# Expert tiles of 64 rows, with two 64-column matmuls side by side, and Pool copies that signal semaphores, in a two-layer MoE trunk

## The reference

```python
def grouped_moe(x, w_router, b_router, w_e_in, w_e_out):
    ...
    expert = g_sel[:, None] * EXPERTS_PER_GROUP + top_i     # two of 16 experts for each token
    weight = top_p / jnp.sum(top_p, axis=-1, keepdims=True)
    flat_e = expert.reshape(-1)
    order = jnp.argsort(flat_e)
    tok = order // TOP_K
    xs = xt[tok]
    group_sizes = jnp.bincount(flat_e, length=N_EXPERTS).astype(jnp.int32)
    h = lax.ragged_dot(xs, w_e_in, group_sizes)             # 1024 -> 2 x 512
    h_gate, h_up = jnp.split(h, 2, axis=-1)
    y = lax.ragged_dot(jax.nn.silu(h_gate) * h_up, w_e_out, group_sizes)   # 512 -> 1024
    y = y * weight.reshape(-1)[order][:, None].astype(y.dtype)
    out = jnp.zeros_like(xt).at[tok].add(y.astype(xt.dtype))
    return out.reshape(B, S, D)
```

## Time and profile before

| | |
|---|---|
| median of 3 runs | 3080.5 us (3073.62 to 3087.33) |
| the profiled execution | 3085.13 us, span 3083.4 us |
| busy share: PE, DVE, ACT, POOL | 91%, 51%, 38%, 9% |
| matmuls | 15876 |
| mean granted TensorE clock | 0.952 |
| data moved | 398.58 MB, 129 GB/s on the mean |

### The profile page before, as it was taken

One profiled execution on the slowest core, in us unless ns is written; L12 is line 12 of the kernel. 1 busy time (PEld: TensorE's weight loads), 2 busy tenths in 40 slices (PEclk: granted clock), 3 DMA queues, 4 the chain that ended last, 5 costly groups with the idle time before them and its releaser, 6 DMA issues.

```text
span 3083.4 us, 47529 instructions
## 1 busy us (share of the span) xinstructions
PE 2802.9 (91%) x15876; PEld 1464.4 (47%) x15877; DVE 1561.9 (51%) x2494; ACT 1162.9 (38%) x1846; POOL 267.5 (9%) x240
## 2 busy tenths in 40 slices
PE   5999999999999599999579999999999995999994
PEld 3555554554444344454345555555544442544452
DVE  3243463344346666656533345633433466577665
ACT  3234413222232166546432444232222321566563
POOL 0000000000000022222310000000000000222223
PEclk8999999999999699999788999999999996999996
DMA  6200001111115488877622000111111254699874
GB/s 254 69 1 28 28 19 51 35 46 41 52 62 198 147 310 306 307 246 258 222 77 69 28 1 28 35 35 35 52 52 52 77 187 181 192 364 331 300 252 143
DMA packets 150903, 398.58 MB, mean 129 GB/s; under 512 B 13700, under 2 KB 58928, under 8 KB 149904
## 3 DMA queue, kind: packets, MB, share of 16 engines
q1 hardware_dynamic: 133104, 327.59, 29.0%
q0 software_dynamic: 14816, 54.12, 7.2%
q10 hardware_dynamic: 2816, 14.68, 1.3%
HBM read 343.91 MB, written 56.63 MB: 130 GB/s over the span
## 4 chain that ended last, share of the span: by engine, by line
PE 73%; issue 8%; DVE 5%; DMA 5%; PEld 3%; ACT 2%; DVEq 2%; POOLq 1%; SPq 1%; POOL 0%; PEldq 0%; ACTq 0%
PE PA L2027 13%; PE PA L1602 10%; PE PA L1603 10%; PE PA L1604 10%; PE PB L2046 6%; PE PC L1583 4%; DMA RA<-x_rows,BR 3%; PE PB L1604 3%; PE PB L1603 3%; PE PB L1602 3%; PE PD L1602 2%; PE PD L1604 1%; PE PD L1603 1%; DMA W<-in_w_in_dram 1%; PE PA L1700 1%
## 5 line engine op out<-in xcount | busy, mean ns | idle before, releaser
L2027 PE MATMUL PA<-XT,RA 128*128 128x512 f16 x2304 | 511.0, 382 | 10.3 <-DVE RA L1019 6.2
L1602 PE MATMUL PA<-XT,W 128*128 128x512 f16 x1216 | 461.8, 380 | 0.7 <-issue 0.7
L1603 PE MATMUL PA<-XT,W 128*128 128x512 f16 x1216 | 461.5, 380 | 0.0
L1604 PE MATMUL PA<-XT,W 128*128 128x512 f16 x1216 | 461.4, 379 | 0.0
L2027 PEld LDWEIGHTS PA<-XT,RA 128*128 128x128 f16 x2304 | 226.3, 98 | 277.7 <-issue 15.0
L1019 DVE SCALAR_TENSOR_TENSOR XT<-OT,XT 128x1024 f16<-128x1024 f32 x256 | 294.7, 1219 | 45.9 <-ACT XT L897 45.9
L1019 DVE SCALAR_TENSOR_TENSOR W<-W 128x512 f16<-128x512 f32 (+2 forms) x320 | 199.6, 660 | 167.2 <-ACT W L671 155.5
L821 ACT ACTIVATE WK<-PA,bT 128x512 f32<-128x512 f32 x128 | 87.9, 687 | 495.9 <-PE PA L1604 495.4
L2046 PE MATMUL PB<-W,WK 128*128 128x512 f16 x1152 | 260.6, 383 | 6.6 <-DVE W L1019 4.4
L897 ACT ACTIVATE XT<-OT 128x1024 f16<-128x1024 f32 x240 | 230.5, 1043 | 41.4 <-issue 41.4
L1248 DVE SCALAR_TENSOR_TENSOR MKV<-WK,PB 128x512 f32<-128x512 f32 x96 | 66.0, 687 | 339.3 <-PE PB L1604 339.3
(11 more groups left out here) (355 smaller groups left out, 4267.2 us busy)
## 6 DMA issues: line engine op xcount, KB each, us to landing
OT<-in_w_e_in_dram SPq DMA_DIRECT2D x256, 512.0 KB, 7.5
RA<-in_w_e_out_dram SPq DMA_DIRECT2D x128, 512.0 KB, 9.2
W<-in_w_in_dram SPq DMA_DIRECT2D x104, 512.0 KB, 4.5
W<-in_w_branch_dram SPq DMA_DIRECT2D x32, 256.0 KB, 4.7
W<-in_w_out_dram SPq DMA_DIRECT2D x16, 512.0 KB, 5.2
x_rows<-RC SPq DMA_DIRECT2D x16, 512.0 KB, 5.4
y_sum<-RC SPq DMA_DIRECT2D x16, 512.0 KB, 5.8
OT<-y_sum SPq DMA_DIRECT2D x16, 512.0 KB, 3.8
```

The lines of the kernel that those rows point to most:

```text
L1602: mm(dst, lhs(0), rhs(0), start=first, stop=False)
L1603: mm(dst, lhs(0), rhs(1), start=False, stop=False)
L1604: return mm(dst, lhs(1), rhs(0), start=False, stop=last)
L2027: q = mm(PA[:, half, :], ROWS[:, a, k * P:(k + 1) * P], EIS[:, b, k, half * HALF:(half + 1) * HALF], start=k == 0 and a + b == 0, stop=k = ...
```

## The change

Expert tiles get `HT` = 64 rows, so that less of a tile is padding. Tiles are taken in pairs: one gather brings 128 rows, which are two tiles (`pair_row`), and one set of 8 transposes turns both; from there on each tile goes by itself, with buffers of its own (index b) in PA, PB, PD, `HIDS`, `HID`, `SIL` and `YROW`. A product of 64 rows uses 64 stationary columns, and the two halves of the outputs are two matmuls that write to PSUM partitions 0 to 63 and 64 to 127 (i = 0, 1). The gate half and the up half of the hidden layer are laid out so that both are spread over the 128 partitions, with 256 columns each. The sizes of the routing's tables follow: `TILES` = 52, `PAIRS` = 26.

PE's order becomes, for a pair j: first_product(2j), transpose_hidden(2j - 1), second_product(2j - 2), transpose_rows(j + 1), first_product(2j + 1), transpose_hidden(2j), second_product(2j - 1). The orders on ScalarE and VectorE follow it. SP loads all twelve chunks of an expert in one go (`load_expert`). POOL's copies of addresses signal semaphores (`at_src`, `at_dst`), for which the indirect DMA waits, and the two drains are gone; each scatter waits until the one before it has landed (`y_st`). `wr` takes its place in `ON`, and `y_st` also serves for the store of `keep_rate`.

```diff
-TILES = 2 * T // P + E
+HT = P // 2
+TILES = 2 * T // HT + E + 4
+PAIRS = TILES // 2
+HF = FE // 2
...
-                with sp.If(loads(sp, 0) < loads(sp, 1)):
-                    load_ei(1, e0 + 1)
-                with sp.Fori(1, last) as i:
-
-                    c0, c1, c2 = loads(sp, i - 1), loads(sp, i), loads(sp, i + 1)
-                    with sp.If(c1 < c2):
-                        load_ei(i + 1, c1)
+                with sp.Fori(0, last * 2 + 1) as h:
+
+                    c0, c1 = loads(sp, h), loads(sp, h + 1)
                     with sp.If(c0 < c1):
-                        load_eo(i, c0)
...
+                        load_expert(h + 1, c0)
...
-                def gather_tile(i):
-
-                    pool.wait_ge(row_tr, g0 + i + l)
-                    nc.gpsimd.tensor_copy(at_row[:, 0:1], src_row[:, bass.ds(i, 1)])
-                    pool.drain()
+                def gather_pair(j):
+
+                    pool.wait_ge(row_tr, g0 + j)
+                    pool.sem_inc(passed, 1)
+                    nc.gpsimd.tensor_copy(at_row[:, 0:1], pair_row[:, bass.ds(j, 1)]).then_inc(at_src, 1)
+                    pool.wait_ge(at_src, g0 + j + 1)
+                    pool.sem_inc(passed, 1)
                     gather(at_row[:, 0:1])
...
-                    pool.wait_ge(y_ev, g0 + i + 2)
-                    nc.gpsimd.tensor_copy(at_row[:, 1:2], src_row[:, bass.ds(i, 1)])
-                    pool.drain()
-                    nc.gpsimd.indirect_dma_start(y_sum, bass.IndirectOffsetOnAxis(at_row[:, 1:2], 0), YROW, None,
+                def add_rows(p, o, b):
+                    h = p * 2 + o
+                    pool.wait_ge(y_ev, (g0 + p) * 2 + (o + 5))
+                    pool.sem_inc(passed, 1)
+                    nc.gpsimd.tensor_copy(at_row[0:HT, 1 + b:2 + b], src_row[0:HT, bass.ds(h, 1)]).then_inc(at_dst, 1)
+                    pool.wait_ge(y_st, (g0 + p) * 32 + (o + 1) * 16)
+                    pool.wait_ge(at_dst, (g0 + p) * 2 + (o + 1))
+                    pool.sem_inc(passed, 1)
+                    nc.gpsimd.indirect_dma_start(y_sum, bass.IndirectOffsetOnAxis(at_row[0:HT, 1 + b:2 + b], 0), YROW[b], None,
...
-                        for a, b in ((0, 0), (0, 1), (1, 0)):
-                            for half in range(2):
-                                q = mm(PA[:, half, :], ROWS[:, a, k * P:(k + 1) * P],
-                                       EIS[:, b, k, half * HALF:(half + 1) * HALF],
-                                       start=k == 0 and a + b == 0, stop=k == KD - 1 and a == 1)
+                        for a, w in ((0, 0), (0, 1), (1, 0)):
+                            for i in range(2):
+                                q = mm(PA[i * HT:(i + 1) * HT, b, :].rearrange("p (g n) -> p g n", g=2),
+                                       ROWP[:, a, k, b, :],
+                                       EIS[:, w, k, :].rearrange("p (g i n) -> p i g n", g=2, i=2)[:, i, :, :],
+                                       start=k == 0 and a + w == 0, stop=k == KD - 1 and a == 1)
...
+                with pe.Fori(1, last) as j:
+                    c0, c1, c2, c3 = (loads(pe, j * 2 + i) for i in (-2, -1, 0, 1))
+                    first_product(j * 2, 0, c2)
+                    transpose_hidden(j, -1, 1)
+                    second_product(j, -2, 0, c0)
+
+                    transpose_rows(j + 1)
+                    first_product(j * 2 + 1, 1, c3)
+                    transpose_hidden(j, 0, 0)
+                    second_product(j, -1, 1, c1)
```

More of the change, by code:

```diff
@@ L887, in _ @@
                 act.sem_inc(passed, 1)
[L888 to L892, removed]
-                    for k in range(KD):
+                near = act.value_load(tab[0:1, TILES + 2:TILES + 3], min_val=E // 2 - 4, max_val=PAIRS - 6)
+                before_last = near + 2
@@ new lines, in next_expert, with next_out @@
+                def next_expert(h):
+                    c0, c1 = loads(act, h), loads(act, h + 1)
+                    with act.If(c0 < c1):
+                        ei_high(h + 1, c0, range(KD))
+                def next_out(p, o):
+                    h = p * 2 + o
+                    c0, c1 = loads(act, h - 1), loads(act, h)
+                    with act.If(c0 < c1):
+                        eo_high(p, o, c0)
+                row_high(0, 0)
+                next_expert(0)
+                row_high(0, 1)
@@ L957, in _ @@
-                with act.Fori(2, last) as i:
-                    act_step(i)
-                store_rows(before_last)
-                hidden_high(last)
-                c0, c1 = loads(act, before_last), loads(act, last)
-                with act.If(c0 < c1):
-                    eo_high(last, c0)
-                store_rows(last)
+                next_expert(1)
+                hidden_high(0, 0, 0)
+                silu(0, 1, 1)
+                row_high(1, 1)
+                next_expert(2)
@@ new lines, in _ @@
+                silu(last, -1, 1)
+                next_out(last, -2)
+                row_high(last, 1)
+                store_rows(near + 1, 1, 1)
+                next_expert(last * 2)
+                hidden_high(last, -1, 1)
+                silu(last, 0, 0)
+                next_out(last, -1)
+                store_rows(near + 2, 0, 0)
+                hidden_high(last, 0, 0)
+                silu(last, 1, 1)
+                next_out(last, 0)
+                store_rows(near + 2, 1, 1)
+                hidden_high(last, 1, 1)
@@ L967, in _ @@
+                next_out(last, 1)
+                store_rows(last, 0, 0)
+                store_rows(last, 1, 1)
                 act.preload_act_table_set("natural_log_exp_and_others")
@@ new lines, in hidden_low, with hidden, next_expert @@
+                def hidden_low(p, o, b):
+                    v.wait_ge(hid_hi, (g0 + p) * 2 + (o + 1))
+                    low_part(HIDS[b][:, 1, :], PD[:, b, 0:HF], SX, HIDS[b][:, 0, :]).then_inc(hid_lo, 1)
+                def hidden(p, o, b):
+                    v.wait_ge(hid_sil, (g0 + p) * 2 + (o + 1))
+                    stt(HID[b], PA[:, b, HF:FE], UN, SIL[b], ALU.mult, ALU.mult).then_inc(hid_ok, 1)
+                def next_expert(h):
+                    c0, c1 = loads(v, h), loads(v, h + 1)
+                    with v.If(c0 < c1):
+                        ei_low(c0, range(KD))
@@ new lines, in _ @@
+                hidden(0, 0, 0)
+                row_low(1, 0)
+                next_expert(1)
+                hidden_low(0, 0, 0)
+                hidden(0, 1, 1)
+                row_low(1, 1)
+                next_expert(2)
+                hidden_low(0, 1, 1)
+                hidden(1, 0, 0)
+                next_out(1)
+                row_low(2, 0)
+                next_expert(3)
+                hidden_low(1, 0, 0)
+                with v.Fori(2, last) as j:
+                    hidden(j, -1, 1)
+                    next_out(j * 2 - 2)
+                    row_low(j, 1)
+                    next_expert(j * 2)
+                    hidden_low(j, -1, 1)
+                    hidden(j, 0, 0)
+                    next_out(j * 2 - 1)
+                    row_low(j + 1, 0)
+                    next_expert(j * 2 + 1)
+                    hidden_low(j, 0, 0)
```

338 lines of the change are left out of this document (182 added, 156 removed).

## The result

The changed kernel takes 3102.18 us (median of 6 runs, 3097.01 to 3109.73), the kernel before 3078.64 us beside it (6 runs): a ratio of 1.0077, interval 1.0057 to 1.0097. It is a little slower, where 3000 us and "faster" had been forecast. The profiled execution took 3097.01 us, with a span of 3095.3.

What follows compares the result with a forecast made beforehand. TensorE, paid per tile, was taken to bound the expert stages. Forty pairs at 704 us plus kept and new waits gave 759 against 855.5; with 10 for routing and 6 for the last scatters, 3000 us, range 2945 to 3075.

Steps and rivals of the forecast that it cites:

- Pairs side by side, 216 ns a pair: PE's two products: two 64-column matmuls cost what one full matmul costs, 7.77 us a tile.
- going between widths: PE, between 64-column matmuls and full-width transposes: three stays a pair of tiles, 0.75 us; bounds nothing and twice that.
- The rule of the Trainium skill: PE's products: loads overlap matmuls only on other array rows, so bare here, 564 us more, 3564; rival's chance 0.05.
- Pool's drains: Pool's gathers: without drains they go out some 7 us earlier, and PE's 18.0 us of waits for late rows go.
- Pool rows whose own time grows: Pool's timeline: a sign that the prediction is wrong, if their own time grows with the drains gone; no size given.
- The rival in which Pool is held by each indirect DMA: Pool's gather and scatters: descriptor work causes the 8 us, 320 more, 3320; turns at 6.1 us a scatter; chance 0.08.
- Loads: SP's weight loads where two-tile experts follow each other: 2 us in seven places, 14 us; bounds nothing and 26.
- the handover at the expert changes: ScalarE, VectorE, then PE passing weight chunks between experts: the likeliest way for the prediction to fail; no separate size.
- Conversions: ScalarE and VectorE converting weights: 0.7 us a three-tile expert, 0.5 a two-tile one, 19 us; bounds nothing and 3 each.
- The rival in which they set the pace: Expert changes: each of 32 costs 3 us in place of 0.6, 77 more, 3077; chance 0.15.
- Routing: Routing ahead of the expert stages: operations on 52 in place of 32, 5 us a layer, 10 in all; bounds 6 and 14.
- The tail: End of each layer: the last scatter waits for the one before, about 3 us, 6 in all.

Runs made afterwards that it cites:

- experiment 6: Changed kernel with each product's left column half computed in full before its right half: 3467.58 us.
- experiment 4: Kernel before, tiles of 128 rows, with semaphores on Pool's index copies in place of its two drains: 3058.00 us, 0.9947 of before.
- experiment 2: Changed kernel with PE's four table values loaded two at the loop's head and two ahead of the odd first product: 3089.37 us, 1.0039 of before.
- experiment 9: Changed kernel with `w_e_in` loads ahead of `w_e_out` loads and each PE table value loaded by itself ahead of its product: 3009.82 us, 0.9772 of before.
- experiments 1 and 5: Each on the changed kernel: the first put `w_e_in` loads ahead of `w_e_out` loads, 3034.96 us; the other put Pool's two drains back, 3157.57 us.

## Why the prediction was wrong

*Pairs side by side, 216 ns a pair: right.* 48 matmuls in 5.30 us, 17.66 us a pair of tiles where nothing waits, for 17.6 forecast; experiment 6 shows that side by side is the cause. Of the 17.66, 15.55 are 72 pairs at 216 ns and 1.31 the transposes at 0.109, so 0.80 is left for going between widths, for 0.75 forecast. The weight loads are hidden. The rule of the Trainium skill that the prediction weighed ("TensorE: Matmul & The Clock Gate", Part 3, what overlaps and what doesn't) does not hold for these pairs.

*Pool's drains: right, and worth more than forecast.* The gathers go out 0.84 us after their copy (L591), PE waits for one, 0.9 us. Worth 20 us in the kernel before and 55 in the changed one. The prediction had named Pool rows whose own time grows as a sign of being wrong, and that came in part: in experiment 4 a scatter is recorded at 2.64 us on the mean, for 1.84 before. But that is far under the 6.1 at which the rival turns the result, and in the changed kernel the median is 1.45. The rival in which Pool is held by each indirect DMA is refuted.

*Loads: the step that failed.* The prediction had seen that "the four second weights, which wait for the conversion of the expert before, stand ahead of the next expert's eight", and then priced it by bandwidth, 19.1 us of transfer against 17.6 of PE: 14 us in seven places, at most 26. The 19.1 us itself was misread (experiment 4): that stretch was slow by late gathers. And the order alone cost 67 us in the median and 73.5 in the stages. What was left out is that a blocked list doesn't only lose bandwidth, it strings latencies together: the `w_e_in` loads can't go before the last `w_e_out` load has gone, which waits for a conversion, nor before SP has read its next table values, 5.2 us, and then conversion, issue, landing, ScalarE's part, VectorE's part and PE's product then follow one another, some 29 us where each resource needs under 20. DMA at a share of 0.71 was the sign. The clock costs too in this run of experts: from 2790.40 to 2797.39, just behind 19 us in which PE was busy for 10.4, the window gives a mean of 0.76, so part of it at 1.2 GHz and part at 2.4, and the 48 matmuls took 6.99 in place of 5.30. The prediction feared for the handover at the expert changes, but with the conversions as the cause.

*What the sum had no term for: PE's own queue.* The kernel before asks for two table values at the head of each turn (`c1, c2`), 1.6 us by the price above, and the matmuls of 128 columns, one per 216 ns, hid them: the earlier trace rows has no gap. The changed kernel asks for four in a row, 3.2 us, and its matmuls come one per 108 ns; 1.2 to 3 us stood bare in a turn. So two things changed at once, and both count: two values in a row, which the kernel before hides, still leave 17.7 us of "issue" ahead of the first product in experiment 2 (23 times, up to 1.3). How the loss divides between them was not tried. Spreading the values gave 13 us by itself, 18 in the stages, and 16 to 18 in the stages behind the mended loads; the doubled values cost 102. The Trainium skill ("TensorE: Matmul & The Clock Gate", Architectural detail) puts TensorE's queue at 64 instructions. As an estimate from it, a weight load and a matmul per 108 ns are 3.5 us of cover where there had been 6.9. The rows agree in kind: 3.2 us of values left 1.3 us bare at 2841.47, which would be 1.9 us of cover, and the queue's depth itself was not measured.

*Conversions: about right.* 19 us forecast; with the loads and values mended, PE's waits for L1082 are 11.7 + 10.7 + 3.0. The rival in which they set the pace is out: the same conversions fit in experiment 9.

*Small terms.* Routing cost 4.5 us a layer, for 5: from its first matmul to the first row transposes 24.81 us (1046.77 to 1071.58), for 20.32 (1048.01 to 1068.33), and in the second layer 24.61 for 20.12. The tail took 4.4 us more in the first layer (24.47 idle, for 20.07) and 5.6 in the second, 10 for 6: the last scatters wait for each other.

With the two causes mended the stages take 769.1 us, for 759 forecast, and the kernel 3010, for 3000. So most of the forecast gain was there; it was given back by one list of transfers (73.5 us of the stages) and one row of register loads (18), and about 10 us stay between forecast and kernel.

## What to carry to other kernels

When loads share an in-order queue, price their order by what each one waits for and not by their bytes: a load whose buffer is free must not stand behind one that waits for a later stage of the work, and the sign of it is that every resource is under its limit while the period grows. When instructions become half as long and register loads stand together at one place, look again at what the queue did for free between them; it shows as idle time ahead of the first instruction of a loop turn. And price a drain behind a small copy by the indirect transfers about it: here 20 us with one scatter a tile, 55 with two a pair. Last, before a slow stretch is put down to bandwidth, look for a wait of the busiest engine in it.

The best version here is the changed kernel with `w_e_in` loads first and the table values spread, 3010 us, 2.3% under the kernel before.

## What the runs showed of the hardware that was not expected

- A table value read into a register of TensorE's queue costs 0.8 us in the loop, though its load is recorded at 0.302 us; up to two register operations of 0.15 and a bounds check of 0.02 are recorded beside it, and the rest isn't recorded. It shows in the profile as "issue", or under the name of whatever semaphore came last.
- 64-column matmuls of one column half only, 512 columns moved, still take 216 ns each; but in a queue of 24 left and 24 right ones some 0.73 us is saved at the seam, where nine start in 1.11 us.
- The profiled runs of experiments 1 and 5 had a mean granted clock of 0.80 between 150 and 200 us, all others 1.00, though the edits touch nothing of PE's there. Both reach their first stage 7 us later than the changed kernel, and such a difference says nothing of the edit, so the stage's own length is the better measure of an edit.
